# Stick-breaking heads: scores in one block behind the values, branch segments regrouped to one and two or three per head

## The reference

```
xn  = RMSNorm(x)
cols = xn @ w_in                      # all projections
pool_y = trailing means, mixed        # branch 0
sb_y   = stick_breaking(q, k, v)      # branch 1: 8 heads x 128
ml_y   = mLSTM(q, k, v, gates)        # branch 2: 4 heads x 256
merged = sum_b sigmoid(gate_b) * ((y_b * silu(z_b)) @ w_branch[b])
x_out  = x + RMSNorm(merged @ w_out)

stick_breaking, per head:
  z     = q k^T / sqrt(128)
  log_1m = log_sigmoid(-z) where key < query, else 0
  after  = reversed cumulative sum of log_1m, exclusive
  a      = exp(log_sigmoid(z) + after) where key < query, else 0
  out    = a v
```

## Time and profile before

| | us |
|---|---|
| median of three runs | 2224.4 |
| the profiled execution | 2225.11 |
| its span, first to last instruction | 2223.3 |
| TensorE busy with matmuls | 2208.7 (99%) |
| VectorE busy | 1539.5 (69%) |
| ScalarE busy | 947.2 (43%) |
| GpSimd busy | 234.8 (11%) |
| mean granted clock of TensorE | 0.999 of full speed |

### The profile page before, as it was taken

How to read it: one execution, slowest core, us unless ns; L and a number is a source line. 1 busy time by engine, 2 the same in 40 slices (tenths; PEclk the granted TensorE clock), 3 DMA queues, 4 the chain that set the end, 5 groups by cost and what they waited for, 6 DMA issues and landing times.

```text
span 2223.3 us, 38578 instructions
## 1 busy us (share of the span) xinstructions
PE 2208.7 (99%) x16186; PEld 2163.9 (97%) x16186; DVE 1539.5 (69%) x1788; ACT 947.2 (43%) x1280; POOL 234.8 (11%) x335
## 2 busy tenths in 40 slices
PE   9999999999999999999999999999999999999998
PEld 7999999999999999999999999999988999999998
DVE  7876768657666667676676666666577577778676
ACT  5343434334444444434444444444555234324543
POOL 0000000000100023323320000000001112100000
PEclk9999999999999999999999999999999999999999
DMA  6444453534444445454545343444765765763448
GB/s 181 116 128 110 111 144 103 150 105 124 122 117 123 131 130 145 122 143 102 142 109 136 108 133 111 129 116 135 236 210 151 250 194 175 189 169 90 130 131 270
DMA packets 426060, 318.04 MB, mean 143 GB/s; under 512 B 13325, under 2 KB 386965, under 8 KB 424480
## 3 DMA queue, kind: packets, MB, share of 16 engines
q1 hardware_dynamic: 403520, 251.18, 41.0%
q0 software_dynamic: 22288, 63.87, 9.2%
q10 hardware_dynamic: 80, 0.52, 0.1%
HBM read 254.53 MB, written 60.99 MB: 142 GB/s over the span
## 4 chain that ended last, share of the span: by engine, by line
PE 96%; DVE 1%; DMA 1%; ACT 1%; issue 0%; POOL 0%; SPq 0%; DVEq 0%; POOLq 0%; ACTq 0%
PE pp L1029 67%; PE pp L1255 12%; PE pp L1431 7%; PE M L1047 2%; PE pp L1039 1%; PE M L1347 1%; PE pp L1528 1%; PE M L1216 1%; PE M L1039 1%; PE M L1368 1%; PE M L1276 1%; PE M L1301 1%; DMA gt_lo<-gated_scratch 1%; PE M L1407 0%; PE pp L1514 0%
## 5 line engine op out<-in xcount | busy, mean ns | idle before, releaser
L1029 PE MATMUL pp<-xa,wa_hi 128*128 128x288 f32 x7392 | 1480.3, 296 | 0.1
L1029 PEld LDWEIGHTS pp<-xa,wa_hi 128*128 128x128 f32 x7392 | 1185.5, 188 | 1.1 <-DVE zs L2170 0.4
L1029 PE MATMUL pp<-xa,wa_lo 128*128 128x288 f32 x3696 | 1086.7, 294 | 0.0
L1029 PEld LDWEIGHTS pp<-xa,wa_lo 128*128 128x128 f32 x3696 | 696.1, 188 | 0.0
L2058 DVE TENSOR_TENSOR wa_lo<-raw_a,wa_hi 128x1024 fp32r<-128x1024 f32 x262 | 319.3, 1221 | 223.5 <-ACT wa_hi L1550 223.4
L1550 ACT ACTIVATE wa_hi<-raw_a 128x1024 fp32r<-128x1024 f32 x262 | 276.7, 1056 | 204.8 <-PE pp L1029 203.8
L2058 DVE TENSOR_TENSOR wa_lo<-raw_r,wa_hi 128x1024 fp32r<-128x1024 f32 x134 | 177.2, 1322 | 147.8 <-ACT wa_hi L1550 147.8
L1550 ACT ACTIVATE wa_hi<-raw_r 128x1024 fp32r<-128x1024 f32 x134 | 141.4, 1055 | 134.0 <-PE pp L1029 126.7
L1255 PE MATMUL pp<-gt_hi,wb_hi 128*128 128x288 f32 x768 | 169.1, 302 | 0.7 <-DMA gt_lo<-gated_scratch 0.7
L1255 PE MATMUL pp<-gt_hi,wb_lo 128*128 128x288 f32 x768 | 164.3, 295 | 0.0
L1255 PE MATMUL pp<-gt_lo,wb_hi 128*128 128x288 f32 x768 | 164.3, 295 | 0.0
(11 more groups left out here) (368 smaller groups left out, 2568.5 us busy)
## 6 DMA issues: line engine op xcount, KB each, us to landing
raw_a<-in_w_in_dram SPq DMA_DIRECT2D x202, 512.0 KB, 5.1
raw_r<-in_w_in_dram SPq DMA_DIRECT2D x68, 512.0 KB, 5.1
z_scratch<-zs POOLq DMA_DIRECT2D x56, 576.0 KB, 3.3
raw_b<-in_w_branch_dram SPq DMA_DIRECT2D x48, 512.0 KB, 4.3
gz<-z_scratch SPq DMA_DIRECT2D x48, 288.0 KB, 4.3
raw_a<-in_w_out_dram SPq DMA_DIRECT2D x20, 512.0 KB, 6.4
gt_hi<-gated_scratch SPq DMA_DIRECT2D x4, 1152.0 KB, 7.4
gt_lo<-gated_scratch SPq DMA_DIRECT2D x4, 1152.0 KB, 10.5
```

Source lines behind the costliest of these rows:

```text
L1029: i = nc.tensor.matmul(out, ws[:, slot, k, :], xa[:, o, part, k, :], start=opens and k == 0 and s == 0, stop=k == HK - 1 and s == 2, skip_ ...
```

## The change

Slots become two per head: one segment after all of scores, and three (heads 2 to 4) or two (heads 5 to 7) after the transposes. Scores stand whole, directly behind the values of the head before. The part of scores from column 1024 on, and the transposes, wait for a new semaphore `sample_gated`, which the 64-column gating counts, and no longer for `g_ready`; `weigh_values` waits for `g_ready`. VectorE's merges move with the segments; `key_weights(7)` goes ahead of `split_lo(17)`. In SP's order the `past_v` of head 7 goes ahead of the first `ml_k`.

```diff
-SB_SLOTS = [[1, 1, 1, 1]] * 3 + [[1, 1, 1, 0]] * 3
+SB_SLOTS = [[1, 3]] * 3 + [[1, 2]] * 3
...
+        sample_gated = sem("sample_gated")
...
             ml_q_in(0)
             ml_gate_rows(0)
+            head_past_v(SBH - 1)
             ml_k_in(0)
-            head_past_v(SBH - 1)
...
-            def scores(i, between=()):
+            def scores(i):
...
                     if col >= SB_BANK:
-                        for h, s in between:
-                            seg(h, s)
                         if i >= 2:
-                            pe.wait_ge(g_ready, PG + i - 1)
+                            pe.wait_ge(sample_gated, i - 1)
...
             def weights_to_keys(i):
...
                 if i:
-                    pe.wait_ge(g_ready, PG + i)
+                    pe.wait_ge(sample_gated, i)
...
             def weigh_values(i):
                 pe.wait_ge(at_read, i + 1)
+                if i:
+                    pe.wait_ge(g_ready, PG + i)
...
             for i in range(2, SBH):
-                scores(i, sb_segs(i, 0))
+                scores(i)
+                for h, s in sb_segs(i, 0):
+                    seg(h, s)
+                weights_to_keys(i - 1)
                 for h, s in sb_segs(i, 1):
                     seg(h, s)
-                weights_to_keys(i - 1)
-                for h, s in sb_segs(i, 2):
-                    seg(h, s)
                 weigh_values(i - 1)
-                for h, s in sb_segs(i, 3):
-                    seg(h, s)
...
             def gate_head(i):
...
-                nc.vector.tensor_tensor(z[:, TP:T], M[:, SB_OUT:SB_OUT + TS], z[:, TP:T], ALU.mult)
+                nc.vector.tensor_tensor(z[:, TP:T], M[:, SB_OUT:SB_OUT + TS], z[:, TP:T], ALU.mult
+                                        ).then_inc(sample_gated, 1)
...
                 logits(i)
-                for h in sb_halves(i, 0):
-                    merge(h)
                 gated_lo(PG + i - 2, zsb[i % 2][:, :])
                 above_zero(i)
                 split_lo(At(2 * i + 2))
-                for h in sb_halves(i, 1):
+                for h in sb_halves(i, 0):
                     merge(h)
                 key_weights(i - 1)
                 sums_from(i)
-                for h in sb_halves(i, 2):
-                    merge(h)
                 exponents(i)
-                for h in sb_halves(i, 3):
+                for h in sb_halves(i, 1):
                     merge(h)
             gate_head(SBH - 2)
+            key_weights(SBH - 1)
             split_lo(At(H_SB + 1))
-            key_weights(SBH - 1)
```

## The result

The changed kernel takes 2228.49 us (median of 22 runs, 2226.16 to 2233.11) against 2224.42 us (22 runs, 2222.84 to 2228.13): a ratio of 1.0018, interval 1.0013 to 1.0024, or +4.07 us. The prediction was 2225.8 us (+1.4) in 2222.9 to 2227.0. The sign is right, the size is a third, and the median lies 1.5 us outside the range.

What follows compares the result with a forecast made beforehand. TensorE, holding a matmul 99% of the span, was taken as the bound. Borders 0.0, head 2 +0.1 (inside the queue's shift), past_v 0 and gt_lo +1.4 gave +1.4 us: 2225.8 us, range 2222.9 to 2227.0 for 8 in 10.

Steps and rivals of the forecast that it cites:

- Part 1: Heads 2 to 7 on TensorE: nine fewer borders between runs of plain matmuls are worth 0.0 us.
- The rival that borders are worth 2.2 us: Idle time in scores' weight loads put at the borders: nine fewer save 2.2 us, giving 2222.2 us; borders gain, chance 0.14.
- Part 2: New order against other engines: +0.1 us at head 2's transposes; scores' wait for the bank stays covered, cost 0.
- The rival of 2230.3 us by a bank wait: Scores of heads 5 to 7, columns from 1024: TensorE waits some 1.5 us in each of three heads; chance 0.04.
- Part 3: Last head and DMA queue: merge(13) behind exponents(7) delays SP's loads, so gt_lo lands 1.4 us later before segment (16, 0).
- The swap: SP's past_v ahead of ml_k in the last head: worth 0 alone, since gt_lo ends the wait.
- its case of +2 to +4: Several tenths more from head 2 or SP make the kernel +2 to +4 us; chance 0.08.

Runs made afterwards that it cites:

- e2: Changed kernel with GpSimd's zml by oml product in all four mLSTM heads held until VectorE has summed the squares; 2228.12 us, ratio 1.0016.
- e7: Changed kernel with the third mLSTM head's GpSimd product cut to a 128x64 strip, the rest left out; 2226.03 us, ratio 1.0009.
- g2: Changed kernel with only 128 columns of x_again blocks 1 to 3 loaded, that part of the result left out; 2227.86 us.
- e6: Kernel before with the third mLSTM head's GpSimd product cut to a 128x64 strip, the rest left out; 2224.54 us, ratio 0.9996.
- e8: Changed kernel with merge(13) back ahead of exponents(7) and the third mLSTM head's product cut to a 128x64 strip; 2225.07 us, ratio 1.0003.
- e4: Kernel before with only VectorE's merge(13) moved behind exponents(7); 2227.32 us, ratio 1.0013.
- g3: Kernel before with merge(13) behind exponents(7) and only 128 columns of x_again blocks 1 to 3 loaded; 2225.93 us.
- g1: Kernel before with only 128 columns of x_again blocks 1 to 3 loaded, that part of the result left out; 2223.48 us.
- e5: Kernel before with only past_v of head 7 put ahead of ml_k; 2224.96 us, ratio 1.0001.
- g4: Changed kernel with filling matmuls ahead of the past_v and gt_lo waits and only 128 columns of x_again blocks 1 to 3 loaded; 2228.07 us.
- e1: Changed kernel with merge(13) of head 7 put back ahead of exponents(7), nothing else; 2226.42 us, ratio 1.0009.
- f2: Kernel before with merge(13) behind exponents(7) and filling matmuls ahead of the past_v and gt_lo waits; 2232.34 us, ratio 1.0030.
- h3: Kernel before with the third mLSTM head's GpSimd product held until the last copy of num, so it runs beside VectorE's sums; 2227.02 us, ratio 1.0009.
- f1: Changed kernel with filling matmuls on TensorE ahead of the past_v and gt_lo waits, no wait removed; 2230.87 us, ratio 1.0020.

## Why the prediction was wrong

**Part 1 (borders, 0.0).** Right: scores' joined row is as long as computed, and a head of three segments takes 16.83 us from scores to scores (1688.79 to 1705.62; 16.82 before, 1689.12 to 1705.94). The rival that borders are worth 2.2 us is refuted.

**Part 2 (+0.1, no bank wait).** Right: no VectorE wait stands inside scores, VectorE stood ready 0.8 us before the gating of head 6 (1 us was computed), and head 2 loses 0.2 us. The rival of 2230.3 us by a bank wait is refuted, though its number is nearer to the result than mine.

**Part 3 (+1.4 at gt_lo).** Right at its place. From scores(1) to the ml_k transposes the five traces in the old order take 156.0 to 156.5 us, the four in the new order with merge(13) late and nothing filled in (the changed kernel, e2, e7, g2) 157.6 to 158.5: +1.6 between their middles. The swap is worth nothing, as forecast. The Trainium skill, "DMA: Bandwidth & Descriptors", section "Queues, rings and completion order", gives ring order with completion not first-in-first-out; past_v, put ahead of ml_k, came down from 8.2 to 7.9 us only the earlier trace rows, and TensorE still waits for it. The trace gives no case against the rule.

**The step that failed** is the last sentence of Part 3: "Everything after it (the mLSTM heads) follows TensorE and shifts with it." It does not. The products on GpSimd start when zml lands, the sums on VectorE when TensorE has finished the numerator, and the two meet or miss each other by a microsecond. Over the stretch from the ml_k transposes to the last matmul the traces give 465.8 us where the product is cut short (e6, e7, e8) and 466.0 where it is whole but starts early enough (e4, g3); 466.3 in g1; 467.4 in the profiled execution of before and 467.5 in e5; 467.9 in the changed kernel, g2 and g4; and 469.6 and 469.5 where the clock fell as well (e1, f2). So the sum lacked a second term, 0.5 us between the two profiled executions and 1.7 us between g1 and g2. It was hidden twice: the profiled execution of before already paid 1.6 us over the shortest stretch (0.9 up to the squares of the third head; of the rest, behind them, I can name only a wait of 0.2), and it stood in the list of waits as a small row of another stage, 0.8 us for the sums.

The account. By the traces of g1 and g2, whose tails are alike: 1.7 us queue and 1.7 us collision, 3.4 in all, of 4.4 between their medians. By the medians of the full kernels: +4.07; undoing the late merge gives 2.1 back, undoing the collision 2.5, both 3.4. Made alone in the kernel before, they cost 2.7 and 2.3, but these two are no measure of the terms, since in both traces (e4, h3) the last matmul starts no later than in the kernel before. That the two together are less than their sum has one reason in the traces: each moves where zml and the sums meet (e4's trace has no wait for the sums at all).

**What stays open.** The traces show 3.4 us (g1 and g2), where the medians differ by 4.1, and by 4.4 in that pair. The clock's fall behind the 1.9 us wait is in two of the five profiles that have that wait (not in the changed kernel, g2 or g4, the last with 1.8); at 1.6 us each it would be 0.6 us on average, which would nearly close the account, but five profiles don't measure a frequency and no run was made that sets it alone. Why zml's load takes 7.8 instead of 6.7 us was not tried either. SP issues it 110.1 us after the ml_k transposes in both kernels, and it stands beside a DMA share of 1.0 to 1.1 in 1860:1870 in both; only the time to landing differs, 5.6 to 8.2 us over all the traces.

**The range** was too narrow in one direction. It took the scatter of my own terms and had nothing for a term of another stage, though two sides in a race (a DMA's landing, an engine's reach) were there to be seen for any shift of 1.4 us. It gave 0.12 to everything above +2 us, and its case of +2 to +4 looked for the cause in head 2 or SP.

## What to carry to other kernels

A shift of the critical engine by a microsecond does not travel unchanged: follow it to the next places where an engine and a transfer race each other, and read the small waits there as the edge of a larger one. Ask too how much stands between the delayed result and its reader: the same collision cost nothing in the second mLSTM head, with 4.0 us from the sums to the squares, and reached TensorE in the third, with 0.8. (Moving work of TensorE in between there was not tried.) When two VectorE operations change places, ask which of them frees a buffer that a queue of loads stands behind; here 0.7 us of work held 4.8 MB. Compare several executions before a difference of 2 us is read from two traces: the waits for past_v and gt_lo in the old order were 1.2 to 2.0 us in five traces. And before a difference of medians is given to a cause, see in the trace whether the last matmul moved with it, or only the tail.

## What the runs showed of the hardware

- VectorE's sum of two SBUF tiles stands still while GpSimd multiplies two: 0.45 us alone, up to 2.89 us beside a product of 2.83 (e1). In e1 the first sum, 0.12 us ahead of the product, took 0.46 and the second the 2.89. VectorE counts as busy meanwhile, so no idle time shows it. VectorE's copies of num and den out of PSUM took the same 0.6 us each beside a product (e4) as without one (e1). The Trainium skill, "SBUF — State Buffer", section "SBUF: two separate sides", says that the pair of ports is locked for a whole instruction, between a GpSimd operation and a VectorE one with two SBUF inputs, and that the other blocks fully; the traces agree, and the wait is up to the product's whole length, 1.9 us of it on TensorE's path.
- The granted clock fell to the lower level for a few microseconds behind a wait of 1.9 us in two of the five profiles with that wait (e1, f2); matmul pairs then start 0.48 us apart instead of 0.27. The waits ahead of segment (16,0), up to 3.1 and 3.2 us long (e4, g3), had no such fall in any trace.
- A mean granted clock of 0.998 instead of 0.999 is no sign of a throttled matmul: 4 us more of a tail without matmuls do it (f1), and e1, whose clock did fall for a few microseconds, has 0.999.
- The reload of 1.5 MB at the end takes 11.9 to 16.6 us in the sixteen traces with all loads, and 6.0 to 6.2 us in the four with 2.4 MB less beside it (g1 to g4).
